# Hybrid block: stick-breaking's triangular sums in two rounded passes on a split softplus, its mask as a product, and another order in the first stage

## What is computed

```
h = rmsnorm(x); p = h @ W_in                     # 3216 columns
A: stick-breaking attention, 6 heads x 64
   z = q k / 8;  mask: key < query
   l = where(mask, log_sigmoid(-z), 0)
   between = reverse_cumsum(l, keys) - l
   weights = where(mask, exp(log_sigmoid(z) + between), 0);  o = weights @ v
B: RWKV-7 time mixing, 6 heads x 64 (generalised delta rule, group norm, gate)
C: gated linear attention (GLA), 4 heads, chunks of 64
y = concat(A, B, C) @ W_out;  x = x + rmsnorm(y)
x = x + rmsnorm(relu(rmsnorm(x) @ W1)^2 @ W2)
```

## Time and profile before

| | us |
|---|---|
| Three runs | 1600.99 to 1603.92, median 1602.38 |
| The profiled execution, its own time | 1599.22 |
| its span (first to last instruction) | 1597.5 |
| TensorE busy (93% of the span) | 1480.6 |
| VectorE busy (45%) | 714.8 |
| ScalarE busy (33%) | 523.5 |
| GpSimd busy (18%) | 286.6 |
| mean granted clock of TensorE | 0.971 |

### The profile page before, as it was taken

How to read it: one execution, slowest core, us unless ns; L and a number is a source line. 1 busy time by engine, 2 the same in 40 slices (tenths; PEclk the granted TensorE clock), 3 DMA queues, 4 the chain that set the end, 5 groups by cost and what they waited for, 6 DMA issues and landing times.

```text
span 1597.5 us, 27221 instructions
## 1 busy us (share of the span) xinstructions
PE 1480.6 (93%) x11233; PEld 1140.8 (71%) x11233; DVE 714.8 (45%) x1152; ACT 523.5 (33%) x936; POOL 286.6 (18%) x304
## 2 busy tenths in 40 slices
PE   5989998889897898898999999999999999999997
PEld 5867777667676554453578788888888888888875
DVE  6455332746562564747265424233242424242336
ACT  4523321333313466766443412112040303121121
POOL 5453523302231162524100100000000000000000
PEclk9999999979998899999999999999999999999998
DMA  5554413313234412003152411202020202112015
GB/s 179 143 151 117 130 49 84 112 55 95 57 87 96 143 34 67 15 2 112 51 180 93 132 40 40 66 13 92 0 97 8 92 13 66 39 39 66 26 40 184
DMA packets 134793, 124.10 MB, mean 78 GB/s; under 512 B 20797, under 2 KB 112122, under 8 KB 134698
## 3 DMA queue, kind: packets, MB, share of 16 engines
q1 hardware_dynamic: 88192, 92.69, 18.7%
q10 hardware_dynamic: 46506, 30.04, 6.8%
HBM read 97.88 MB, written 24.84 MB: 77 GB/s over the span
## 4 chain that ended last, share of the span: by engine, by line
PE 45%; DVE 2%; ACT 1%; DMA 1%; issue 1%; POOLq 0%; SPq 0%; DVEq 0%; ACTq 0%
PE all_ps_b L1933 22%; PE all_ps_b L1910 21%; PE all_ps_b L1515 2%; DMA bk_acc<-in_w_out 1%; POOLq L1535 0%; DVE bk_acc L1798 0%; PE all_ps_b L1903 0%; ACT bk_acc L1701 0%; DVE bk_acc L1808 0%; DVE bk_w1L L1769 0%; DVE bk_acc L1794 0%; DVE all_hL L1814 0%; DVE bk_acc L1865 0%; DVE bk_acc L1868 0%; DVE all_gL L1840 0%
## 5 line engine op out<-in xcount | busy, mean ns | idle before, releaser
L1850 DVE TENSOR_TENSOR bk_acc<-bk_acc,all_ps_b 128x512 f32<-128x512 f32 x128 | 87.9, 687 | 283.6 <-PE all_ps_b L1933 283.6
L1910 PE MATMUL all_ps_b<-all_hH,bk_w1L 128*128 128x512 f32 x512 | 200.1, 391 | 5.1 <-PE all_ps_b L1933 2.1
L1933 PE MATMUL all_ps_b<-bk_w2H,all_gL 128*128 128x512 f32 x512 | 199.3, 389 | 2.5 <-DVE all_gL L1840 2.5
L1910 PE MATMUL all_ps_b<-all_hH,bk_w1H 128*128 128x512 f32 x512 | 199.3, 389 | 0.0
L1910 PE MATMUL all_ps_b<-all_hL,bk_w1H 128*128 128x512 f32 x512 | 199.2, 389 | 0.0
L1933 PE MATMUL all_ps_b<-bk_w2L,all_gH 128*128 128x512 f32 x512 | 199.2, 389 | 0.0
L1933 PE MATMUL all_ps_b<-bk_w2H,all_gH 128*128 128x512 f32 x512 | 199.2, 389 | 0.0
L1155 PE MATMUL fr_ps_F<-fr_hH,fr_wL 128*128 128x512 f32 (+1 forms) x416 | 174.8, 420 | 0.0
L1155 PE MATMUL fr_ps_F<-fr_hH,fr_wH 128*128 128x512 f32 (+1 forms) x416 | 164.4, 395 | 0.8 <-issue 0.8
L1155 PE MATMUL fr_ps_F<-fr_hL,fr_wH 128*128 128x512 f32 (+1 forms) x416 | 164.9, 396 | 0.0
L1680 ACT CAST bk_w2H<-all_raw 128x1024 fp32r<-128x1024 f32 x32 | 32.9, 1048 | 355.2 <-PEq L1938 351.7
(11 more groups left out here) (333 smaller groups left out, 2350.6 us busy)
## 6 DMA issues: line engine op xcount, KB each, us to landing
fr_raw<-in_w_in ACTq DMA_DIRECT2D x37, 512.0 KB, 4.2
bk_raw<-in_w_ff SPq DMA_DIRECT2D x32, 512.0 KB, 4.3
all_raw<-in_w_ff SPq DMA_DIRECT2D x32, 512.0 KB, 4.8
projected<-fr_stage ACTq DMA_DIRECT2D x39, 256.0 KB, 4.5
fr_raw<-in_w_in SPq DMA_DIRECT2D x13, 512.0 KB, 4.1
fr_xt<-in_x SPq DMA_DIRECT2D x8, 512.0 KB, 5.3
bk_acc<-in_x SPq DMA_DIRECT2D x8, 512.0 KB, 3.4
x_after_mixers<-bk_acc SPq DMA_DIRECT2D x8, 512.0 KB, 2.6
```

What stands on the lines that cost most here:

```text
L1850: dve.tensor_tensor(acc[:, j, ds], acc[:, j, ds], ybank[g % 4][:], ALU.add).then_inc(collected, 1)
L1910: m = pe.matmul(bank[s][h][:], w[s][:, k, :], a[:, k, hs], start=(k == 0 and q == 0), stop=(k == KB - 1 and q == 2))
L1933: m = pe.matmul(ybank[g % 4][:], a[:, i, ts], w[:, i, ds], start=(i == 0 and q == 0), stop=(i == FB - 1 and q == 2))
```

## The change

In the first stage:

- FILL: p4 has 21 steps instead of 14, g1 of group 0 has 9 instead of 16.
- GpSimd's subtraction for the low part of a weight block is four instructions of two key blocks each (256 elements a partition).
- The 16 x 16 inversion: both 8 x 8 diagonal corners are inverted at once, in 7 steps of a product and a reduction, and the upper right corner is made by two 8 x 8 x 8 products, each a product of 512 elements and a reduction.
- ScalarE's `late` is parted: `inverse_norms` stays between g1 and g2, `decays` (three exponentials) comes behind the copy of "rt16".
- VectorE: `cumulate` comes behind L998, `keys`, `bvec` and `avec` behind "r32", `rk_product` and `rtilde` behind `ktilde`, ahead of label u.

In the attention stage:

- The softplus is no longer masked by VectorE. On a diagonal unit TensorE adds to z, by a third f32r matmul of 128 columns (identity times an array that holds -1e30 where masked and 0 elsewhere), what makes the exponentials zero; the mask product and GpSimd's select go.
- GpSimd copies SP into SPH (f32r) ahead of its running sum; VectorE makes SPL = SP - SPH behind GLA's piece of the unit (`low`). SP has three buffers, SPH and SPL two each.
- The triangle is f32r. `sums` does the ones matmul first (waiting for cut, log and sp), then the triangle times SPH, then the triangle times SPL.
- `values` no longer waits for cut.

The core of the diff:

```diff
-            "p3": (16,), "p4": (14,), ... "g1": (16, 4, 4, 6),
+            "p3": (16,), "p4": (21,), ... "g1": (9, 4, 4, 6),
...
-                pool.tensor_tensor(wL[b][:, :, 0:wd], raw[b][:, :, 0:wd], wH[b][:, :, 0:wd].bitcast(F32), ALU.subtract
+                for k in range(0, KB, 2):
+                    m = pool.tensor_tensor(wL[b][:, k:k + 2, 0:wd], raw[b][:, k:k + 2, 0:wd],
+                                           wH[b][:, k:k + 2, 0:wd].bitcast(F32), ALU.subtract)
+                m.then_inc(s(f"w_low{b}"), 1)
...
-                R = inverse[:]
-                for t in range(1, B16):
-                    dve.tensor_tensor(work16[:, 0:t, 0:t], R[:, 0:t, 0:t],
-                                      mine[:, 0:t, t].unsqueeze(1).to_broadcast([P, t, t]), ALU.mult
-                    dve.tensor_reduce(R[:, 0:t, t], work16[:, 0:t, 0:t], AX.X, ALU.add
+                R, N = corners(inverse[:]), corners(mine[:])
+                for t in range(1, B8):
+                    w = work8[:, 0:2, 0:t, 0:t]
+                    step(lambda: dve.tensor_tensor(w, R[:, :, 0:t, 0:t], N[:, :, 0:t, t].unsqueeze(2)
+                                                   .to_broadcast([P, 2, t, t]), ALU.mult)).then_inc(s("column"), 1)
+                    step(lambda: dve.tensor_reduce(R[:, :, 0:t, t], w, AX.X, ALU.add)).then_inc(s("column"), 1)
+                def by_rows(to, left, right):
+                    step(lambda: dve.tensor_tensor(work8[:], left.unsqueeze(2).to_broadcast([P, B8, B8, B8]),
+                                                   right.rearrange("p l t -> p t l").unsqueeze(1)
+                                                   .to_broadcast([P, B8, B8, B8]), ALU.mult)).then_inc(s("column"), 1)
+                    return step(lambda: dve.tensor_reduce(to, work8[:], AX.X, ALU.add))
+                by_rows(middle[:], mine[:, 0:B8, B8:B16], inverse[:, B8:B16, B8:B16]).then_inc(s("column"), 1)
+                by_rows(inverse[:, 0:B8, B8:B16], inverse[:, 0:B8, 0:B8], middle[:]).then_inc(s("inverse"), 1)
...
@@ VectorE, core(i)
-                    cumulate(i + 1)
                 serve(i, "g1", "g2", "g3")
...
-                    keys(i + 1)
-                    bvec(i + 1)
+                    cumulate(i + 1)
                 serve(i, "h", "z1")
                     amod(i + 1)
-                    avec(i + 1)
                 add_to_r("r32", "r16")
+                    keys(i + 1)
+                    bvec(i + 1)
+                    avec(i + 1)
                 serve(i, "z2")
...
                     ktilde(i + 1)
+                    rk_product(i + 1)
+                    rtilde(i + 1)
...
@@ attention, GpSimd
+                    pool.tensor_copy(SPH[u % 2][:, span(u)], SP[(i * NU + u) % 3][:, span(u)]).then_inc(s("sp_high"), 1)
                     if kb > 0:
                         ... running sum as before
-                    if kb >= PER * c:
-                        pool.wait_ge(s("weight"), i * NU + u + 1)
-                        pool.affine_select(out=w, in_=w, compare_op=ALU.is_gt, fill=0.0, base=0,
...
@@ attention, VectorE
+                def low(u):
+                    dve.wait_ge(s("sp_high"), i * NU + u + 1)
+                    if u >= 2 or i:
+                        dve.wait_ge(s("tri_mm"), i * NU + u - 1)
+                    dve.tensor_tensor(SPL[u % 2][:, span(u)], SP[(i * NU + u) % 3][:, span(u)],
+                                      SPH[u % 2][:, span(u)].bitcast(F32), ALU.subtract).then_inc(s("sp_low"), 1)
...
                     gla(i * NU + u)
+                    low(u)
...
@@ attention, TensorE
+                    if kb >= PER * c:
+                        m = pe.matmul(Z[u % NZ][:, off:off + P], unit[:], never[:], start=False, stop=True,
...
-                    m = pe.matmul(z, tri[:], SP[u % 4][:, span(u)], start=False, stop=True, skip_group_check=True)
                     if not first:
                         pe.wait_ge(s("cut"), i * NU + u - 1)
+                        pe.wait_ge(s("log"), i * NU + u + 1)
+                        pe.wait_ge(s("sp"), i * NU + u + 1)
                         pe.matmul(z, ones[:], rd[:, span(u)], start=False, stop=True, skip_group_check=True)
+                    pe.wait_ge(s("sp_high"), i * NU + u + 1)
+                    pe.matmul(z, tri[:], SPH[u % 2][:, span(u)], start=False, stop=True, skip_group_check=True)
+                    pe.wait_ge(s("sp_low"), i * NU + u + 1)
+                    pe.matmul(z, tri[:], SPL[u % 2][:, span(u)], start=False, stop=True, skip_group_check=True
+                              ).then_inc(s("tri_mm"), 1)
```

98 lines of the change are left out of this document (49 added, 49 removed), and 2 rows, old and new, of the table FILL.

## The result

The changed kernel takes 1641.64 us (median of 6 runs, 1637.74 to 1643.16), the kernel before 1601.68 (6 runs beside them): ratio 1.0245, 95% interval 1.023 to 1.0259. It is slower by 2.5%; forecast were 1583 us and a range to 1605. The profiled execution has a span of 1640.2 us, against 1597.5. The attention stage begins where TensorE first turns a value block: 541.5 us before, 538.1 after. It ends, at the last unit's weight, at 775.5 and 817.3. So the first stage gained 3.4 of the 29 us forecast, the attention stage lost 41.8 + 3.4 = 45 where 10 were forecast, and the rest is as long as before to within 1 us (822.9 us, before 822.0).

What follows compares the result with a forecast made beforehand. TensorE, busy about nine tenths of both changed stages, was taken as the bound. First stage -29 and attention +10 gave -19 against the profiled 1599.2, so 1580; the runs' median lies 3.2 higher, so 1583 us, range 1559 to 1605.

Steps and rivals of the forecast that it cites:

- Last pair's full units 3.65: Attention stage, last pair: split, copy, running sum and low follow one another on the shared port, 3.65 us a full unit.
- Sixteen full units of the first two pairs stay TensorE's: -6.4: Attention stage: TensorE still bounds these units, where GLA's matmuls lie, so its shorter passes save 6.4 us.
- Twelve GLA key steps, 12 times 1 us: Attention stage: low(u) stands behind key steps that wait for ScalarE, costing 1 us each, +12 us.
- Rival (b): Attention stage: the ring of softplus, copy, sum and low in every unit, 0.55 us each, 40 in all; 1613 us, chance 0.13.
- each running sum followed by a low of over 1.2 us: Attention stage: a sign that the forecast is right, with GpSimd's sum taking the port before VectorE's low.
- Mask product -4: Attention stage: dropping VectorE's mask product saves 4 us of TensorE's waits; TensorE's 48 mask passes cost 5.
- Inversion: First stage: the blocked inversion takes 7.5 us instead of 12.0, so TensorE waits 14 us less for the inverted blocks.
- the clock's term of 6 us: First stage: shorter pauses raise TensorE's granted clock, 6 us won at the second pause, 11 over all, bounds 0 and 20.
- The pieces: First stage: GpSimd's quarter subtractions may each let a VectorE product pass, delaying the weights' low part, 1.5 us lost.
- Given back +7: First stage: the new order and pieces lose 7 us together, 2.5 of them at the first group's half-turned activations.
- rival (c): First stage doesn't pay: pieces starve TensorE, keys come late for "r64"; it wins 5, attention costs 10; 1607 us, chance 0.15.
- The two other waits: First stage: 21 steps in p4 cover a 4.6 us wait before the first group; moving the scan's product saves 4.3.

Runs made afterwards that it cites:

- e2: Kernel before with the change's attention stage alone, first stage as before: 1642.4 us (one execution), attention stage 275.7 us.
- e7: e2 with VectorE's subtraction low(u) left out, TensorE's second pass reading the rounded part again: 1594.0 us (one execution), attention stage 225.3 us.
- e3: e2 with VectorE doing low(u) ahead of GLA's piece of the unit instead of behind it: 1632.1 us (one execution).
- e5: e3 with GpSimd's running sum made to wait until low(u) is done: 1621.8 us (one execution).
- e8: e3 with the rounded copy made by VectorE instead of GpSimd, and GpSimd's sum waiting for low(u): 1609.9 us (one execution).
- e4: e2 with GpSimd's running sum made to wait until low(u) is done, low(u) still behind GLA's piece: 1647.0 us (one execution).
- e11: Kernel before with the blocked inversion alone: 1591.17 us, ratio 0.9929.
- e14: Kernel before with the blocked inversion, the 21 steps in p4, and GpSimd's subtraction in four pieces from the 21st weight block on: 1580.55 us, ratio 0.9852.
- e1: Kernel before with the change's whole first stage alone, attention stage as before: 1598.97 us, ratio 0.9997.
- e10: e1 without the new order of VectorE's and ScalarE's operations (inversion, 21 steps and all pieces kept): 1587.13 us, ratio 0.991.
- e13: Kernel before with the blocked inversion and the 21 steps in p4, old order, whole subtraction: 1586.61 us, ratio 0.9911.

## Why the prediction was wrong

The attention stage decided. Point by point, by the forecast's own steps.

**"Last pair's full units 3.65."** Right: 3.45, by the mechanism named, GpSimd first at the port. The pair's loss was 9.1 us in the changed kernel and 9.6 in e2, 7.5 forecast. The rule of the Trainium skill (SBUF — State Buffer, Who interferes with whom) that the first to issue holds the port pair for its whole instruction agrees with low's 1.75 us and, where VectorE's products are queued, with the turns taken at 112; that GpSimd's next instruction wins where VectorE waits for a semaphore is what the earlier trace rows said, and the trace confirms it in each full unit of the last pair.

**"Sixteen full units of the first two pairs stay TensorE's: -6.4."** This step failed, by 22 of the 35 us that the stage was off: these units lost 15.8 us (37.07 and 35.13 us for the two stretches of eight, before 28.72 and 27.73). The premise was right, TensorE did fill them before. The conclusion wasn't: e7 shows that 2.1 and 2.4 us less of TensorE's work shorten them by only 0.1 and 0.7, since another path of nearly the same length lies under it; and low lengthens that path or makes one of its own. In e2 the stretches are 6.2 and 8.8 us longer than before, in e3, with low first, 7.2 and 7.8. I took "TensorE is busy nine tenths" for "a shorter sum shortens the unit", and took GLA's work beside the ring for a cover, though on VectorE (1.1 to 1.3 us a piece) and on GpSimd it stands in the ring. The clock is the other thing left out: it was 0.86 and 0.90 in the two stretches, 1.00 before, and over the stage TensorE's work got 13 us longer instead of shorter, at 0.86 where it was 0.94. The forecast has a term for the clock in the first stage and none here.

**"Twelve GLA key steps, 12 times 1 us."** In part. The row exists, as at 603, but key steps stand ahead of only 6.6 of TensorE's 42.7 us of waits for low, in seven waits; the two longest, 10.0 us together, are at GLA's output norm, which the forecast had nowhere. e3 gave 12.7 us back, but it moves low ahead of all of GLA's pieces, so that this is near 12 is luck. Outside the last pair and the sixteen full units the first two pairs lost 20.2 us, 8.5 forecast.

**Rival (b)**, the ring in every unit, at +40, is in size what came, and that is luck in part. Its ring, low beside GpSimd's sum, runs in 18 of the 72 units, so the sign "each running sum followed by a low of over 1.2 us" held in a quarter of them; in the others low stands mostly behind GLA's work, another row. Its price of 0.55 us a unit is an average of 0.13 to 0.2 in the first eight units of the first and third pair, 0.7 to 0.9 in those of the second, and 0.8 to 1.1 in the full ones of the first two pairs. Its argument "every GLA piece now stands ahead of TensorE's last pass" was the right one. By runs the 45 us are: 12.7 the place of low (e3), 8.4 the port (e5, which needs e3), 10.7 the copy on VectorE in place of the hand-over (e8), 18.6 the remainder's own work and what is left of its waits (e8 to e7), less the 4.9 that the scheme then gains; each order of the steps would share them out otherwise, as e4 shows.

**"Mask product -4"** for VectorE, and 5 us for TensorE's 48 short passes: together +1 was forecast, and -3.8 came (0.9976; -5.4 by the stage). The first term fits the fall of TensorE's waits for softplus by 6 us; that the second came to nothing because TensorE waits in those units anyway is argued, and no run takes it apart.

**Inversion.** Its own time was right (7.5 forecast; 7.4 to 7.8 us in the later groups, 9.3 in the first). "14 us less" of waits was mis-sized: alone it took 1 us off the blocks' waits and 1.7 off the norms', and gained 9 by the medians. Of the clock's term of 6 us at this pause, a gain of 1.4 to 2.2 us behind it is what e11 shows against six of the nine executions of the old first stage; against the other three, before among them, it is 5.8 to 6.3, but those differ from the six by about 4 us without any change. So the row on which the term was built was one execution's clock. At the other pauses nothing of it is seen. What I left out is that the blocks' return meets GpSimd's next whole subtraction.

**The pieces**, "1.5 us", were the step of the first stage that failed. The mechanism stood in the text (a piece lets a product pass); the price was 7.3 us of TensorE's waits for the low part (the 6.5 shown and 0.8 at another product), 6.6 of them ahead of 200 us. I put that down to the place: the preparation of the first group has the densest row of VectorE products and the weight blocks nearest to their due time. "Given back +7" for the order named one place rightly: its 2.5 us for the half-turned activations are the 2.6 to 2.7 us that these waits grow by in every run with the order. As a net price it was mis-sized: beside whole blocks the order costs 1.5 us by the medians (or nothing), beside the pieces 12. So of rival (c), that the first stage doesn't pay, the pieces' part is shown; "keys come late" is shown in that one wait, and nothing was found at "r64".

**The two other waits.** The 21 steps: -4.6 by the medians, -4.6 forecast. The scan's wait: 4.3 to 1.7.

Without the order and with the first 20 blocks whole, the first stage gains 20 us (e14's median), still not 29. The first stage's forecast thus failed by the pieces in the first 20 blocks and their meeting with the order (18 us by the medians, e1 against e14), and what is left of the gap lies in the blocks' waits (13.7 to 5.5 in e14) and the 11 us for the clock; it isn't taken apart.

## What to carry to other kernels

Before a busy engine's work is cut, look for the path that comes next in length, and for the ring that the change makes, and walk both through every queue with the neighbour's work standing in it. Here softplus, copy, remainder and another mixer's piece summed to more than TensorE's unit; and even with the remainder for nothing a saving of over 2 us on a TensorE that was busy throughout gave 0.1 and 0.7. A subtraction whose operand another engine must first round costs two hand-overs here, and both engines' order (what stands ahead of it, what the partner issues next) has to be laid down by hand. Cutting a long instruction on a shared port into pieces helps the other engine and delays its own result, so cut it only where its consumer has time: the same edit lost 6.6 us in the first 20 blocks (e10 against e14) and gained 6.1 in the rest (e14 against e13); both are medians of four and five runs, with intervals that meet. And before a price is read from one execution's clock, look at a second execution of the same code.
